# Two chain steps and two level steps in each group of 64x64 products: six groups in an iteration of block 2's recurrence where there were twelve

## What is computed

```python
def _rwkv7_scan(r, decay, k, v, kk, b):
    def step(state, inp):
        r_t, w_t, k_t, v_t, kk_t, b_t = inp
        sk = jnp.einsum('bhvk,bhk->bhv', state, kk_t)
        state = (state * w_t[:, :, None, :] - sk[..., None] * b_t[:, :, None, :]
                 + v_t[..., None] * k_t[:, :, None, :])
        return state, jnp.einsum('bhvk,bhk->bhv', state, r_t)
```

## Time and profile before

| what | value |
|---|---|
| median of three runs | 1196.23 us |
| the profiled execution's own time | 1198.47 us |
| its span in the profile | 1196.7 us |
| PE busy | 1160.9 us, 97% |
| DVE busy | 495.0 us, 41% |
| ACT busy | 215.0 us, 18% |
| iteration j = 0, from its first product to the next iteration's first | 44.94 us |
| an iteration j = 1 to 6 | 51.1 us |
| iteration j = 7 | 34.09 us |

### The profile page before, as it was taken

How to read it: one execution, slowest core, us unless ns; L and a number is a source line. 1 busy time by engine, 2 the same in 40 slices (tenths; PEclk the granted TensorE clock), 3 DMA queues, 4 the chain that set the end, 5 groups by cost and what they waited for, 6 DMA issues and landing times.

```text
span 1196.7 us, 19636 instructions
## 1 busy us (share of the span) xinstructions
PE 1160.9 (97%) x8368; PEld 954.3 (80%) x8368; DVE 495.0 (41%) x1232; ACT 215.0 (18%) x545; POOL 79.8 (7%) x119
## 2 busy tenths in 40 slices
PE   6999999999999999999999899999999999999997
PEld 5888888878888487777676787888888888877886
DVE  3333242524342020000000576766776667766332
ACT  2122130312100010000001322212122221223101
POOL 1100000000023000000000110110101101020000
PEclk9999999999999979999999899999999999999999
DMA  6335638172556245344441733232232322151230
GB/s 233 135 135 179 248 124 303 56 262 110 201 143 185 94 152 193 124 176 141 159 158 71 239 102 96 85 105 90 89 107 84 95 90 72 36 195 54 89 123 36
DMA packets 50570, 160.48 MB, mean 134 GB/s; under 512 B 5394, under 2 KB 10418, under 8 KB 50484
## 3 DMA queue, kind: packets, MB, share of 16 engines
q1 hardware_dynamic: 49764, 158.12, 38.5%
q10 hardware_dynamic: 720, 1.11, 0.3%
HBM read 158.11 MB, written 1.10 MB: 133 GB/s over the span
## 4 chain that ended last, share of the span: by engine, by line
PE 91%; DVE 4%; DMA 4%; ACT 0%; issue 0%; SPq 0%; DVEq 0%
PE bank L377 37%; PE bank L677 21%; PE bank L586 9%; PE bank L831 3%; PE bank L985 2%; PE bank L509 2%; DMA arena<-in_ada_w 2%; PE bank L818 2%; DVE arena L1657 1%; PE bank L656 1%; PE bank L712 1%; DMA slots<-in_w_heads 1%; PE bank L662 1%; PE bank L445 1%; PE bank L780 1%; PE bank L389 1%
## 5 line engine op out<-in xcount | busy, mean ns | idle before, releaser
L377 PE MATMUL bank<-hT,slots 128*128 128x256 f32 x1760 | 390.5, 382 | 5.8 <-DMA slots<-in_w_heads 3.8
L377 PEld LDWEIGHTS bank<-hT,slots 128*128 128x128 f32 x1760 | 335.5, 192 | 59.5 <-issue 9.7
L677 PE MATMUL bank<-hT,slots 128*128 128x256 f32 x1152 | 275.0, 386 | 1.2 <-DVE arena L1727 0.8
L677 PEld LDWEIGHTS bank<-hT,slots 128*128 128x128 f32 x1152 | 211.5, 190 | 31.8 <-issue 2.0
L1657 DVE SCALAR_TENSOR_TENSOR arena<-padA,par,arena 128x256 f32<-128x256 f32 x232 | 110.3, 532 | 0.0
L586 PE MATMUL bank<-slots,arena 128*128 128x512 f32 x240 | 105.0, 592 | 0.0
L377 PE MATMUL bank<-arena,slots 128*128 128x256 f32 x432 | 93.9, 379 | 0.0
L377 PEld LDWEIGHTS bank<-arena,slots 128*128 128x128 f32 x432 | 82.1, 190 | 11.2
L586 PEld LDWEIGHTS bank<-slots,arena 128*128 128x128 f32 x240 | 45.6, 190 | 52.3 <-issue 51.7
L1550 DVE SCALAR_TENSOR_TENSOR arena<-arena,bank 128x256 f32<-128x256 f32 x22 | 9.3, 421 | 137.0 <-ACT arena L1121 137.0
L1462 DVE SCALAR_TENSOR_TENSOR adaA<-arena,sc,adaA 128x1024 f32<-128x1024 f32 x24 | 30.7, 1283 | 78.6 <-DMA arena<-in_ada_w 78.4
(11 more groups left out here) (306 smaller groups left out, 1159.5 us busy)
## 6 DMA issues: line engine op xcount, KB each, us to landing
slots<-in_w_rwkv SPq DMA_DIRECT2D x72, 512.0 KB, 3.5
slots<-in_w_heads SPq DMA_DIRECT2D x68, 512.0 KB, 7.7
slots<-in_w_gu SPq DMA_DIRECT2D x44, 512.0 KB, 4.4
arena<-in_ada_w SPq DMA_DIRECT2D x24, 512.0 KB, 4.5
slots<-in_w_down SPq DMA_DIRECT2D x22, 512.0 KB, 3.9
slots<-in_w_br SPq DMA_DIRECT2D x32, 256.0 KB, 2.7
slots<-in_w_out SPq DMA_DIRECT2D x16, 512.0 KB, 5.6
slots<-in_w_y SPq DMA_DIRECT2D x16, 512.0 KB, 4.5
```

The costliest lines, as they stand in the source:

```text
L377: end = e.matmul(psum, w[:, k * P:(k + 1) * P], rhs[:, k, :], start=k == 0, stop=k == kt - 1)
L677: end = e.matmul(proj(w, q), slot[w][:, k * P:(k + 1) * P], hT[:, k, :], start=k == 0, stop=k == KT - 1)
```

## The change

Twelve groups become six. A group now has a chain step, a level step, one or two score products that were elsewhere, a second chain step and a second level step, and then 11 to 13 matmuls. In iteration 8, which has chain steps only, nothing is regrouped.

```diff
-FILL = (0, 6, 6, 5, 6, 6, 6, 6, 6, 6, 6, 6, 7)
-FILL_FIRST = (14, 4, 5, 4, 5, 5, 5, 5, 4, 5, 5, 5, 6)
-FILL_LAST = (0, 3, 3, 2, 3, 3, 3, 2, 2, 3, 3, 3, 2)
+FILL = (0, 12, 11, 12, 11, 13, 13)
+FILL_FIRST = (14, 9, 9, 10, 10, 10, 10)
+FILL_LAST = (0, 6, 5, 5, 5, 5, 6)
...
             def outcome(c):
                 e.wait_ge(*dve.upto(f"U{c}.{p}"))
+                if c == 0:
+                    e.wait_ge(*act.upto(f"tok.{p}"))
...
+            def between():
+                if not levels:
+                    fill(next(n))
...
             if levels:
-                e.wait_ge(*act.upto(f"eT.{j}"))
-                e.wait_ge(*dve.upto(f"R.{j}"))
-                to_tokens(e, chunks(bank[4][:, 0:T]), Bf, cst2_of("unit"))
-                to_tokens(e, chunks(bank[4][:, T:]), Kf, cst2_of("unit")).then_inc(*pe.step(f"tok.{j}"))
+                e.wait_ge(*dve.upto(f"A.{j}"))
...
-            fill(gaps[1])
+            between()
             if chain:
                 solved(0)
             if levels:
                 if j > 2:
                     e.wait_ge(*act.upto(f"gn.sd.{j - 3}"))
-                products(e, chunks(half(5)), Kf, Af[j % 2]).then_inc(*pe.step(f"M.{j}"))
-                e.wait_ge(*act.upto(f"tok.{j}"))
-                products(e, chunks(bank[4][:, 0:T]), Bf, Rf[j % 3])
-                products(e, chunks(bank[4][:, T:]), Kf, Rf[j % 3]).then_inc(*pe.step(f"RBK.{j}"))
-            fill(gaps[2])
+                e.wait_ge(*dve.upto(f"rkr.{j}"))
+                e.matmul(half(5), C("pair"), t1, start=True, stop=True).then_inc(*pe.step(f"bonus.{j}"))
+            fill(next(n))
             if chain:
                 outcome(0)
             if levels:
                 grown(1)
-                e.wait_ge(*dve.upto(f"RBK.{j}"))
-                if more:
-                    low_rank_mm(e, j + 1).then_inc(*pe.step(f"low.{j + 1}"))
-                e.matmul(half(5), C("pair"), t1, start=True, stop=True).then_inc(*pe.step(f"bonus.{j}"))
+                products(e, chunks(bank[6][:, T:]), K, A).then_inc(*pe.step(f"M.{j}"))
...
-            fill(gaps[3])
+            between()
             if chain:
                 forced(1)
             if levels:
                 inverted(1)
-            fill(gaps[4])
+            if more:
+                low_rank_mm(e, j + 1).then_inc(*pe.step(f"low.{j + 1}"))
+            fill(next(n))
             if chain:
                 solved(1)
             if levels:
                 grown(2)
-            fill(gaps[5])
+                e.wait_ge(*dve.upto(f"bonus.{j}"))
+                e.wait_ge(*dve.upto(f"R.{j}"))
+                products(e, chunks(bank[5][:, 0:T]), B, Rf[j % 3])
+            between()
             if chain:
                 outcome(1)
             if levels:
                 inverted(2)
```

On DVE the reads follow PE's order, and the taps are dealt out anew: 18 to 27 after the first group (9 to 19 in iteration 0), 27 to 31 and the next pair's 0 to 4 after the second (19 to 31 in iteration 0), 4 to 10, 10 to 13 and 13 to 18 after the third, fourth and sixth. The order around rkr:

```diff
                 e.wait_ge(*pe.upto(f"N1.{j}"))
                 e.tensor_tensor(Xs, chunks(half(3)), each(cst2_of("off_first")), ALU.mult).then_inc(*dve.step(f"X0.m.{j}"))
+                e.scalar_tensor_tensor(out=t1, in0=rT, scalar=PC("r_k", j), in1=kp, op0=ALU.mult, op1=ALU.mult).then_inc(*dve.step(f"rkr.{j}"))
+            if chain:
+                solved(0)
+            if levels:
                 e.wait_ge(*dve.upto(f"X0.m.{j}"))
                 e.tensor_tensor(Xs, Xs, each(cst2_of("unit")), ALU.add).then_inc(*dve.step(f"X0.{j}"))
-                e.scalar_tensor_tensor(out=t1, in0=rT, scalar=PC("r_k", j), in1=kp, op0=ALU.mult, op1=ALU.mult).then_inc(*dve.step(f"rkr.{j}"))
...
+                e.wait_ge(*pe.upto(f"bonus.{j}"))
+                e.tensor_tensor(bonus[j % 3], vT, half(5), ALU.mult).then_inc(*dve.step(f"bonus.{j}"))
+                taps(e, j, 18 if j else 9, 27 if j else 19)
```

Work moves from DVE to ACT. The shift of r, k and v was a subtraction and a multiply-add on DVE; now ACT writes `(1 - mu) * z` while it writes z into its padded row, and DVE does one multiply-add. The scaled key and its square (two DVE operations) become one ACT square and a multiply inside an operation that was there; `t1` of the key's gate moves to ACT:

```diff
             e.activation(pads[n][:, 1:], proj(w, j), ACT.Copy).then_inc(*act.step(f"pad.{n}.{j}"))
+            m = j + 8 * "rkv".index(n)
+            e.activation(XW[n], proj(w, j), ACT.Copy, scale=omu[:, m:m + 1]).then_inc(*act.step(f"own.{n}.{j}"))
...
-        def shift_d(e, n, j):
-        def shift_s(e, n, j):
-        def kk_squares(e, j):
+        def shift(e, n, j):
+        def act_keys(e, j):
+        def act_a(e, j):
```

More of the change, by code:

```diff
@@ L668, in projection @@
             e.wait_ge(*in_slot[w].upto(f"rw{w}.{q}"))
[L669 to L675, removed]
+            read_out(e, n - 2)
             for k in range(KT):
@@ L688, in layer_sum @@
                 e.wait_ge(*act.upto("ln.sq"))
+            read_out(e, PLACE[w, LAST] - 2)
             for k in range(KT):
-                end = e.matmul(half(4), ones, src[:, k, :], start=k == 0, stop=k == KT - 1)
+                end = e.matmul(proj(w, LAST), ones, src[:, k, :], start=k == 0, stop=k == KT - 1)
                 if k == KT - 1:
-                    end.then_inc(*pe.step(name))
+                    end.then_inc(*pe.step("ln.sum" if w == LNSUM else "ln.var"))
                 yield
@@ L892, in pe_rwkv @@
                 grown(3)
-                fill(2)
-                e.wait_ge(*dve.upto(f"bonus.{j}"))
-                if j > 1:
-                    e.matmul(bank[5][:, T:], C("pair"), osq, start=True, stop=True).then_inc(*pe.step(f"gn.var.{j - 2}"))
-                if more:
-                    e.wait_ge(*dve.upto(f"kk.sq.{j + 1}"))
-                    e.matmul(half(5), C("pair"), rn, start=True, stop=True).then_inc(*pe.step(f"kk.sum.{j + 1}"))
-                fill(gaps[7] - 2)
-            else:
-                fill(gaps[7])
+                products(e, chunks(bank[5][:, T:]), K, Rf[j % 3]).then_inc(*pe.step(f"RBK.{j}"))
+            between()
             if chain:
@@ L906, in pe_rwkv @@
                 inverted(3)
-            fill(gaps[8])
+                fill(4)
+                e.wait_ge(*dve.upto(f"RBK.{j}"))
+                if j > 1:
+                    e.matmul(bank[5][:, T:], C("pair"), osq, start=True, stop=True).then_inc(*pe.step(f"gn.var.{j - 2}"))
+                if more:
+                    e.wait_ge(*act.upto(f"kk.sq.{j + 1}"))
+                    e.matmul(half(5), C("pair"), rn, start=True, stop=True).then_inc(*pe.step(f"kk.sum.{j + 1}"))
+                fill(next(n) - 4)
+            else:
+                fill(next(n))
             if chain:
@@ L1254, in act_rwkv @@
                 faded(2)
+            if levels:
+                inverted(2)
             if more:
                 act_decays(e, j + 1)
+                act_keys(e, j + 1)
                 act_pad(e, "r", R_, j + 1)
+            if last:
+                half_gate(ROG, rg[j % 3], "rg.th", j)
+            if levels:
+                inverted(3)
+            if more:
                 act_kk(e, j + 1)
@@ L1759, in dve_rwkv @@
                 grown(1)
-            if more:
-                dve_decays(e, j + 1)
-            if levels:
-                taps(e, j, 26 if j else 21, CONV2)
-                join_taps(e, j)
             if chain:
@@ L1769, in dve_rwkv @@
                 inverted(1)
-                e.wait_ge(*pe.upto(f"bonus.{j}"))
-                e.tensor_tensor(bonus[j % 3], vT, half(5), ALU.mult).then_inc(*dve.step(f"bonus.{j}"))
+                e.wait_ge(*pe.upto(f"M.{j}"))
+                e.tensor_tensor(Mt[j % 2], chunks(bank[6][:, T:]), each(cst2_of("st")), ALU.mult).then_inc(*dve.step(f"M.{j}"))
+            if more:
+                dve_decays(e, j + 1)
+            if levels:
+                taps(e, j, 27 if j else 19, CONV2)
+                join_taps(e, j)
             if more:
@@ L1863, in dve_rwkv @@
                 grown(5)
+                inverted(5)
             if more:
```

221 lines of the change are left out of this document (104 added, 117 removed).

## The result

| | before | after |
|---|---|---|
| median of the runs | 1196.33 us (11) | 1206.26 us (11) |
| ratio, 95% interval | | 1.0068 [1.0048, 1.0087] |
| profiled execution, its span | 1198.47, 1196.7 us | 1206.37, 1204.5 us |
| mean granted clock of TensorE | 0.989 | 0.981 |
| iteration 0 | 44.94 us | 49.79 us |

The change makes the kernel 0.7% slower; 1196.5 us was forecast, in a range of 1191.5 to 1201. The six middle iterations gained 3.75 us. The two edges and what follows lost 4.85, 3.05 and 4.13 us; less the gain that is 8.3 us.

The account below looks back on a forecast made before the run. PE, busy 97% of the span, was taken to bound the kernel. Iterations 1 to 6 -2.4, iteration 0 +2.3, iteration 7 +0.4 sum to +0.3 us: 1196.2 + 0.3 = 1196.5 us, range 1191.5 to 1201.

Parts of the forecast that it names:

- Borders, 0.33 us a group: PE's changes of tile shape: each removed group saves 0.33 us, six in each of 8 iterations, 15.8 us gained.
- forecast 0.2 in all: Waits within PE's groups, inverted behind grown's read: 0.1 to 0.3 us an iteration, taken as 0.2.
- The rival by which the borders save nothing: PE's group borders: the loss belongs to the products, half of 15.8 us goes, 1204 us; chance 0.04.
- The bonus wait, 1.4 us: PE's bonus matmul closing group 1 waits for DVE's rkr: 1.4 us an iteration, 9.8 for seven.
- rkr's 0.95 us: DVE's rkr beside POOL: length 0.95 us taken from its earlier row, setting the bonus matmul's start.
- the 1.25: Bonus matmul's wait if rkr waits for POOL's operation until 902.38, then runs 0.48 us: 1.25 us.
- Middle iterations, 50.7 us: Iterations 1 to 6: -2.0 + 1.4 + 0.2 = -0.4 us each, -2.4 together, 50.7 us an iteration.
- just in time; but for PE's wait at the bonus matmul it would be late: Group 2: DVE gives forced(1)'s state at 8.3 us from N1's end; PE needs it at 8.65.
- the slower rival: DVE's taps after group 1 run slower, forced(1) waits 0.65 us in six iterations: +6 us, 1202; chance 0.19.
- Iteration 0, +2.3 us: Iteration 0: stalls 7.45 us in place of 2.7, less 2.0 of groups, +2.75; followed through +2.0; taken +2.3.
- Iteration 7, +0.4 us: Iteration 7: forced(1) loses 2.25 us, sum +0.55; taken as +0.4 since DVE is lighter later.
- I take nothing for it, up to 0.5: Closing iteration, not regrouped: DVE's layer norm moved later costs nothing, up to 0.5 us.

Follow-up runs that it names:

- bonus3_taps: Changed kernel with the bonus matmul behind the filling's third matmul and three of DVE's nine taps moved into the iteration before; 1199.70 us, ratio 1.0011 to before.
- bonus3: Changed kernel with the bonus matmul behind the third matmul of the filling instead of at its head; 1207.48 us, ratio 1.0074 to before.
- warm: Changed kernel with unread 64x64 products put ahead of PE's long waits in iterations 0, 7 and 8; 1201.04 us, ratio 1.0018 to before.
- lnswap: Changed kernel with the last gate projection ahead of the layer norm's second sum in iteration 8; 1201.69 us, ratio 1.0024 to before.
- early_taps: Changed kernel with eight of iteration 0's taps moved into DVE's idle time before it; 1199.42 us, ratio 1.0007 to before.
- fills: lnswap with the filling of iterations 0 and 7 dealt out anew and ACT's gate read of iteration 0 earlier; 1195.10 us, ratio 0.9990 to before.
- best2: best with iteration 7's filling dealt 7, 5, 4, 5, 5, 6; 1190.62 us, ratio 0.9945 to before.
- best: Changed kernel with fills and bonus3_taps together; 1191.33 us, ratio 0.9954 to before.

## Why the prediction was wrong, point by point

Two steps of the prediction failed. It priced each wait of PE at its own length, with no term for what TensorE's clock does behind a wait: 6.4 us. And it put iteration 8 at nothing, where PE waited 2.5 us. The other terms came out within 1.4 us each:

- **Borders, 0.33 us a group.** Held. Iterations of 51.21 us became 49.49 where no wait of 0.3 us or more was left; with the short waits inside the groups (in bonus3_taps 0.08 at inverted(1) and 0.11 in group 4, forecast 0.2 in all) that is 1.9 for six, 0.32 a border. The rival by which the borders save nothing is out.
- **The bonus wait, 1.4 us.** Right in place and number, too large: by the profile 1.08 in five iterations, 0.98 in two, 1.17 in iteration 0; 8.5 us in all instead of 11. The step that took rkr's 0.95 us from the row of before was mis-sized: part of that length was a wait for POOL, and the order of the change alters it. In eight pairs of rows (rkr and X0 of iterations 0, 1, 2 and 4) the DVE operation ends 0.27 to 0.29 us after POOL's. With POOL's end at 902.38 in the earlier trace rows that is 902.67 for rkr, 0.06 more for PE, less 901.65: 1.08. By the same reckoning, from 0.05 us after N1's end, iterations 1 and 2 measured 1.06, and iterations 3 to 7, with their additional wait, 1.15. The Trainium skill, "SBUF — State Buffer", section "SBUF: two separate sides", says that of VectorE and GpSimd the one that comes second to their shared port pair is blocked until the other's instruction ends, and these rows agree with it; the 1.25 that the prediction got from it put the whole 0.48 of a tap behind POOL's end, where the trace has 0.29.
- **Middle iterations, 50.7 us.** 50.6 measured. Together with iteration 1's shorter one, the gain was 3.75 us, not 2.4. DVE's nine taps do stand just behind (bonus3): the step "just in time; but for PE's wait at the bonus matmul it would be late" was right, and the slower rival built on it did not come, as no iteration from 1 to 6 waited for them in after.
- **Iteration 0, +2.3 us.** Measured +4.85. Without the clock, as in warm, it is +3.2, 0.9 over the forecast. The first waits came where forecast, 1.17 and 1.95 us instead of 1.45 and 1.9. In place of 3.35 at inverted(2), PE at full clock waits 1.3 us for ACT's read of the gate projection and then 2.2 at inverted(2) (in warm, three unread products of 0.47 and the 0.80 shown above); the prediction had put ACT's part at nothing. The clock adds 1.6 us.
- **Iteration 7, +0.4 us.** Measured +3.05. forced(1) waited 2.09 us, forecast 2.25; the clock behind it took 3.2 us, forecast nothing; without it the iteration is at -0.15, 0.55 under the forecast.
- **Iteration 8, "I take nothing for it, up to 0.5".** This step failed outright: PE's sum of the squares came before ACT's squares, 2.5 us of waiting and 1.6 of clock. The chain from PE's first sum of the norm, which had moved back in the filling, over DVE to ACT's two 1.06 us squares, and the DVE group norm for which ACT waited ahead of them, had to be followed to the PE matmul that reads the squares.

In sum: the forecast of +0.3, less 1.35 in the middle iterations, plus 0.9 in iteration 0, less 0.55 in iteration 7, plus 2.5 for the wait of iteration 8 and 6.4 for the clock, is 8.2, of 8.3 measured by stages. That the sum without these last two, -0.7, lies near the forecast is partly luck, since its terms are off in both directions. No rival had the clock. That the clock is the cause is shown by warm for its removal by activity alone; that behind the same wait of 2.09 us the slow stretch costs 3.2 us in after, half of that in lnswap and nothing in early_taps is shown too, but what decides between the three is open. The Trainium skill, "TensorE: Matmul & The Clock Gate", Part 1, says that in three kernels the gate's trace events showed these two levels only, and that the number of slow matmuls varies between runs of one kernel. The windows within the slow stretches of after show 0.50 (712.5 to 715.5, 1064 to 1070 and 1094.6 to 1097.6 us), which agrees with the two levels; the three runs here are three kernels, so they do not show what one kernel does from one execution to the next.

## What to carry to other kernels

Merging small groups on the bound engine is worth the lost change of shape (0.33 us here), but it takes the cover off every read in between, so first move the reader's other work (here taps) out of the stretch before the reads and into its idle time, and put filling ahead of the one matmul that waits. Price a wait of some 2 us on a TensorE that was busy throughout at its length and, as an upper end, 1.5 times that again for the clock (3.2 us behind 2.09 here), unless another wait behind it takes the slow stretch in. And where a moved step feeds another engine, follow it to the matmul that reads the end of that chain, also in the last iteration.

## What was not expected of the hardware

- In this kernel one and the same wait of 2.09 us was followed by a stretch at 1.2 GHz that cost 3.2 us, 1.6 us or nothing (after, lnswap and early_taps, iteration 7), and a wait of 2.02 us by no fall at all (fills and best2, iteration 0), while a wait of 1.47 us was once followed by one (best, iteration 0: a clock of 0.86 from 712 to 724 us). Waits of 1.08 us once in 50 us never were: the clock is 1.00 in all windows of iterations 1 to 6 that were read. Nor were the two of 1.3 us in before.
- A slow stretch ahead of a wait for another engine costs nothing: in iteration 0 of after the first of two did not move inverted(2), which begins 21.30 us into the iteration with it (after) and without it (warm).
- A DVE operation on two SBUF inputs that begins while POOL is at work ends 0.28 us after the end of the POOL operation that ran when it began (rkr, X0 and 39 taps between 690 and 1060 us of after, all within 0.277 to 0.285 us; of the taps in bonus3_taps, five that began in the last 0.1 us of a POOL operation do not follow this), whatever its own duration in the rows says (0.54 to 0.95 us): its length depends on where it falls in POOL's series. DVE's read of `bank` beside the same series (X0.m) takes 0.42 us, as such a read (L1750) takes when POOL is idle.
- The nine DVE operations ahead of the state read, which nobody had waited for, bounded PE as much as the one operation that the profile named: with the named wait of 1.08 us gone, PE waited 0.72 to 0.84 us behind them.
